# Addressing of the cache_win0 and cache_win1 copies in a one-step hybrid decoder layer

## What is computed

```
z      = rmsnorm(x) @ w_in                       # 42 mixing chunks, then 4 gates of 2048 channels
merged = sum_b sigmoid(gate_b) * (o_b @ p_b)     # four branches a, b, c, d
x      = x + rmsnorm(merged @ w_o)
x      = x + rmsnorm(conv_gated_mlp(rmsnorm(x)))
```

```
new_len = min(win, W + T)
new_buf = concatenate([buf, stack([k, v], 2)], 1)[:, W + T - new_len:]
```

## Time and profile before

| | us |
|---|---|
| median of 3 runs | 2317.19 (2314.57 to 2317.42) |
| the profiled execution: its span, first to last instruction | 2311.6 |
| PE busy | 2108.5 (91%) |
| DVE, ACT, POOL busy | 1114.1, 773.3, 81.7 |
| merge stage, about | 674 to 1280 |
| channel MLP, about | 1421 to 2240 |

### The profile page before, as it was taken

The page is one execution under the profiler, slowest core; times in us unless marked ns, Lnnn a source line. Parts: engine busy times, 40 slices in busy tenths (PEclk is TensorE's granted clock), DMA queues, the critical chain, the costliest instruction groups (busy, mean ns, idle before and its releaser), DMA issues.

```text
span 2311.6 us, 36850 instructions
## 1 busy us (share of the span) xinstructions
PE 2108.5 (91%) x14921; PEld 1934.4 (84%) x14921; DVE 1114.1 (48%) x1108; ACT 773.3 (33%) x643; POOL 81.7 (4%) x172
## 2 busy tenths in 40 slices
PE   7999977899987996987969896999999999999995
PEld 5999965344457996987969895999999999999995
DVE  4333334355542442423424337565556555655564
ACT  3333333233332332323323332433333333333332
POOL 0000011000000000000000001100000000000000
PEclk9999987899989998998989998999999999999998
DMA  6544521677644654546546641555545454455531
GB/s 219 178 163 163 168 75 25 194 201 203 186 154 151 231 177 168 200 154 229 167 176 206 206 164 43 168 168 168 165 163 163 163 163 163 164 166 167 167 117 55
DMA packets 189396, 377.00 MB, mean 163 GB/s; under 512 B 8985, under 2 KB 33841, under 8 KB 188250
## 3 DMA queue, kind: packets, MB, share of 16 engines
q1 hardware_dynamic: 184300, 340.50, 46.0%
q10 hardware_dynamic: 5015, 35.31, 4.1%
HBM read 365.43 MB, written 37.66 MB: 174 GB/s over the span
## 4 chain that ended last, share of the span: by engine, by line
PE 83%; DMA 7%; DVE 5%; ACT 2%; issue 1%; SPq 0%; ACTq 0%; DVEq 0%
PE ps L1492 23%; PE ps L1494 23%; PE ps L1493 23%; DMA w_raw<-in_p_b 7%; PE ps L1474 4%; PE ps L1695 3%; DVE w_lo L1008 1%; PE ps L1480 1%; DVE m_T L1025 1%; PE ps L1798 1%; ACT w_hi L704 1%; PE ps L1799 1%; PE ps L1810 1%; PE ps L1807 1%; PE ps L1813 0%
## 5 line engine op out<-in xcount | busy, mean ns | idle before, releaser
L1008 DVE TENSOR_TENSOR w_lo<-w_raw,w_hi 128x2048 fp32r<-128x2048 f32 (+1 forms) x272 | 614.7, 2260 | 854.9 <-ACT w_hi L704 854.9
L1492 PE MATMUL ps<-xn_hi,w_hi 128*128 128x288 f32 x3104 | 917.0, 295 | 27.5 <-DVE xn_lo L1031 13.8
L1494 PE MATMUL ps<-xn_hi,w_lo 128*128 128x288 f32 x3104 | 918.1, 296 | 0.0
L1493 PE MATMUL ps<-xn_lo,w_hi 128*128 128x288 f32 x3104 | 916.3, 295 | 0.0
L704 ACT ACTIVATE w_hi<-w_raw 128x2048 fp32r<-128x2048 f32 (+1 forms) x272 | 514.3, 1892 | 1128.2 <-PE ps L1494 1009.7
L1492 PEld LDWEIGHTS ps<-xn_hi,w_hi 128*128 128x128 f32 x3104 | 584.6, 188 | 31.9 <-DVE xn_lo L1031 15.4
L1493 PEld LDWEIGHTS ps<-xn_lo,w_hi 128*128 128x128 f32 x3104 | 584.6, 188 | 0.0
L1494 PEld LDWEIGHTS ps<-xn_hi,w_lo 128*128 128x128 f32 x3104 | 584.6, 188 | 0.0
L1492 PE MATMUL ps<-act_hi,w_hi 128*128 128x288 f32 x704 | 207.8, 295 | 2.8 <-DVE act_lo L1393 2.8
L1494 PE MATMUL ps<-act_hi,w_lo 128*128 128x288 f32 x704 | 208.4, 296 | 0.0
L1493 PE MATMUL ps<-act_lo,w_hi 128*128 128x288 f32 x704 | 208.0, 295 | 0.0
(11 more groups left out here) (274 smaller groups left out, 1699.3 us busy)
## 6 DMA issues: line engine op xcount, KB each, us to landing
w_raw<-in_w_in SPq DMA_DIRECT2D x104, 1024.0 KB, 5.1
w_raw<-in_w_up SPq DMA_DIRECT2D x88, 1024.0 KB, 5.0
w_raw<-in_w_down SPq DMA_DIRECT2D x44, 1024.0 KB, 5.1
kv<-in_cache_k SPq DMA_DIRECT2D x64, 256.0 KB, 2.9
kv<-in_cache_v SPq DMA_DIRECT2D x64, 256.0 KB, 2.9
w_raw<-in_w_o SPq DMA_DIRECT2D x16, 1024.0 KB, 5.1
kv<-in_cache_win SPq DMA_DIRECT2D x16, 512.0 KB, 6.4
out<-in_cache_win ACTq DMA_DIRECT2D x4, 2032.0 KB
```

The lines of the kernel that those rows point to most:

```text
L1008: e.tensor_tensor(w_lo[s][:, 0:k, 0:n], w_raw[slot][:, 0:k, 0:n], w_hi[s][:, 0:k, 0:n].bitcast(F32), ALU.subtract).then_inc(lo_ready, 1)
L1492: e.matmul(dst, w_hi[s][:, r, cols], x_hi[:, k0 + r, :], start=first and r == 0, stop=False)
L1493: e.matmul(dst, w_hi[s][:, r, cols], x_lo[:, k0 + r, :], start=False, stop=False)
L1494: mm = e.matmul(dst, w_lo[s][:, r, cols], x_hi[:, k0 + r, :], start=False, stop=last and r == k - 1)
```

## The change

The source and the destination of a copy are computed first. For window 0 and window 1 both are then rearranged: each of the two sequences' runs is seen as one flat run, cut into 16 equal pieces, and the piece index is made the outermost dimension, ahead of the sequence. For window 1 the shape so becomes 16 x 2 x 16,256 floats (65,024 bytes a piece), for window 0 16 x 2 x 3,968 floats (15,872 bytes a piece). The bytes that move, the number of copies, their order, their queue and their semaphore stay as they are. Window 2 keeps its form.

```diff
@@ -900,8 +900,13 @@
                 g, n0, nb = ((1, 0, 2), (2, 0, 1), (2, 1, 1), (0, 0, 2))[b]
                 first = NT if g < 2 else 0
-                e.dma_start(o[9 + g][0, bass.ds(i * 2 + n0, nb), 0:WIN_LEN[g] - first],
-                            d[f"cache_win{g}"][0, bass.ds(i * 2 + n0, nb), first:WIN_LEN[g]]).then_inc(copied, 16)
+                kept = WIN_LEN[g] - first
+                dst = o[9 + g][0, bass.ds(i * 2 + n0, nb), 0:kept]
+                src = d[f"cache_win{g}"][0, bass.ds(i * 2 + n0, nb), first:WIN_LEN[g]]
+                if g < 2:
+                    dst, src = (a.rearrange("a l v h e -> a (l v h e)").rearrange("a (q f) -> q a f", q=16)
+                                for a in (dst, src))
+                e.dma_start(dst, src).then_inc(copied, 16)
                 hi(unit_no(U_MIX, 20, i, 5 * b + 6))
```

## The result

The changed kernel takes 2231.43 us in the median of 4 runs (2226.89 to 2234.09), the kernel before 2317.31 (2314.57 to 2317.43) beside it. The ratio is 0.9625, 95% interval 0.9611 to 0.9639: 85.9 us less.

What follows compares the result with a forecast made beforehand. PE bounds the kernel nearly everywhere, except while it stalls for p_b behind the window 1 copy. Span 2311.6 - 85.9 = 2225.7 us, plus 5.6 us between span and median, gives 2231.3 us; range 2222 to 2241.

Steps and rivals of the forecast that it cites:

- The bound and the place: Merge stage: PE sets the pace nearly everywhere, but waits near 19 us four times, once a round, for p_b.
- Two engines before, 16 after: Copy of cache_win1: its 32 packets sit on 2 DMA engines before, and go over 16, 2 to each, after.
- 2.5 us a packet: Copy of cache_win1: each 65,024-byte packet takes 2.5 us of an engine; 16 in a row make p_b's 40 us.
- SP's issues: SP's queue behind p_b: the next four issues take 41.18 us together, and go back to 0.37 us each.
- `p_b` lands in 8.2 us: Merge stage: new landing time of the p_b load, 8.2 us in place of 40.4, taken from the load of p_d.
- The limit of 21.5 us: Merge stage: p_b may land up to 21.5 us after its issue before PE waits, 19.5 plus 2.0 us more covered.
- The gain, read from the rounding rows: ACT's rounding rows in the merge stage: four rounds lose 22.05, 20.86, 21.92 and 21.04 us, 85.9 us in all.
- Window 0 is worth nothing: Copy of cache_win0, some 10 us on two engines: p_a's 9.4 us landing is already hidden, so faster gains nothing.
- the 5.6 us between span and median: Whole kernel: 5.6 us added to the forecast span of 2225.7 us to give the median of 2231.3 us.
- the first: Rival, window 1 copy: sequences put outermost again in lowering, so it stays on 2 engines; 2317.2 us, chance 0.03.
- second: Rival, window 1 copy: 16 engines get less from HBM and part of the stall stays; 2285 us at 70 GB/s, chance 0.03.
- The third: Rival, merge stage: a copy longer than 38 us on all engines delays all loads; 2370 us at 40 GB/s, chance 0.01.

Runs made afterwards that it cites:

- e6: Changed kernel without any copy of cache_win1 (those 4 transfers left out): 2231.68 us, ratio 0.9638 to the kernel before.
- e3: Against the changed kernel: window 1 copied per sequence as 2 combs of 8 pieces, comb outermost, window 0 as before the change: 2315.87 us, ratio 0.9995.
- e4: Against the changed kernel: window 1 copied per sequence as 4 combs of 4 pieces, on four engines, window 0 as before the change: 2232.75 us.
- e8: Against the changed kernel: window 1 copied per sequence on two engines, only 10 of 16 pieces, window 0 as before the change: 2260.14 us, ratio 0.9745.
- e2: Changed kernel with only the cache_win0 copy in 16 pieces, cache_win1 left as two runs: 2316.03 us, ratio 0.9999 to the kernel before.
- e10: Against the changed kernel: window 1 copied per sequence on two engines in 8,128-byte pieces, window 0 as before the change: 2297.43 us, ratio 0.9923.

## Why the prediction was right, step by step

- **The bound and the place** (four waits of PE behind `p_b`): right. Without this copy the kernel runs as fast as with it in 16 pieces (e6), and with the copy on two engines the whole stall is back (e3).
- **Two engines before, 16 after:** right. q10's small packets go from 2 to 16 a copy, and the 2.08 MB pass within 10 us; the copy lands in 8.6 us, where the prediction had about 7. The landing times of e3 (outermost 2), e4 (4) and the changed kernel (16) lie on one line when 2, 4 and 16 engines are put in; that is the rule of the Trainium skill (DMA: Bandwidth & Descriptors, Rules for kernel authors), and the runs agree with it.
- **2.5 us a packet:** a little too high; the slope over 2, 8, 10 and 16 packets is 2.35 us.
- **SP's issues:** misread. The "41.18 us together" are the length of a row that joins four issues, with SP's waits for buffers in it. One issue was held, for 19.86 us; the others took 0.37 us before as after. No term of the sum rested on it.
- **`p_b` lands in 8.2 us:** 7.4 was measured (7.0 to 7.9). The landing of `p_d` was a good stand-in. Its exact size didn't matter, since it lies far under the limit. `p_a` landed in 3.8 us, just under the 4 to 6 forecast.
- **The limit of 21.5 us:** right to some tenths. At 21.6 us (e4) PE waits 0.2 us a round, at 26.0 (e8) 4.7.
- **The gain, read from the rounding rows:** 22.05 + 20.86 + 21.92 = 64.8 us was forecast for the three rounds between the first and the last `p_b`. Before they take 1156.56 - 710.69 = 445.9 us (the last `p_b` before is issued at 1156.56) and after 1098.65 - 716.84 = 381.8, so 64.1 were gained. From the first load of `p_b` to the first of `w_o`, all four rounds, it is 536.3 us before and 451.2 after, so 85.1; behind that the two traces differ by 0.4 us. That the medians differ by 85.9 us to the digit is luck, since the interval of the ratio allows 84 to 90 us.
- **Window 0 is worth nothing:** right (e2).
- **What was wrong:** "the 5.6 us between span and median" as what lies around the span. The changed kernel's profiled execution took 2234.09 us with a span of 2232.3, so only 1.8 us lie around it; the execution profiled before must have been a quick one, some 4 us under the median. The forecast of the median stood on the median less the loss and so was not touched, but that of the span (2225.7) missed by 6.6 us, most of it ahead of the merge stage, where the clock dipped. The range of 2222 to 2241 held all four runs, though its upper part was for waits at b = 1 that did not come.
- **The rivals:** the first and second fell with 16 engines and 2.08 MB within 10 us. The third needs a copy longer than 38 us; it lands in 8.6.

## What to carry to other kernels

A transfer that nobody waits for can still set the pace, if it queues tens of microseconds of work on a few DMA engines: every other load has a share on those engines. When one load lands far later than its equals, look at the DMA share and the packet sizes during the wait: here 10 to 11%, a little under 2/16, pointed to a transfer on two engines. Give such a copy one flat run or an outermost dimension of 16, keep its packets large enough that its issue stays short, and work out from the buffers how late a load may land before anything waits.

## What the runs showed of the hardware beside that

- An engine that carries a copy and loads from two queues alternates between them packet by packet. From 738 to 744 before the change it is 4 large packets of the copy for 4 small ones of the loads. With 65 KB packets each one queued on the engine adds 2.35 us to a load's landing (2 to 16 packets). With 8 KB packets on the same two engines, `p_b` landed in 17.1 us, but the loads behind it took up to 37.5 us, and the kernel won back only 19 of the 86 us (e10).
- Issue time isn't constant. Two copies of 16 data packets each took 1.57 us of ACT's queue, 256 packets together 1.75, and 508 together 10.9. Whether that is the building of many packets or a full queue behind it was not tried.
- After 4.4 to 5.1 us of idling PE lost 1.5 to 2.9 us more to the low clock (e8, rounding rows less the wait), after 19 us 1.9 to 3.0 us (before): nearly the same price.
- The granted clock dipped to 0.89 for a stretch of the attention stage in some executions and not in others, also of the same kernel (0.89 and 0.97). The first `p_b` came between 709.4 and 717.2 us with it, and the runs of one kernel spread over 3 to 10 us.
